# Sliding-window attention of a two-layer decoder: heads in pairs, one pair deeper, with the row maxima first

## The chip, the cores and the metric

The kernel is one program on one core of a Trainium2 chip. Its engines are TensorE (PE in the profile, with its weight loads as PEld), VectorE (DVE), ScalarE (ACT), GpSimd (POOL) and SyncE (SP), which issues DMAs. Each engine runs its own instructions in the order in which they are written; between engines they are ordered by semaphores. The metric is the time of one execution on the device in microseconds, of which the median over the runs is given; lower is better.

## The reference

Two layers run over a prompt of 128 tokens and a sample of 512 tokens, 1024 wide. The even layer mixes two branches: attention over 8 query heads of 64 with 2 key heads, and a gated delta rule in 4 heads of 128. The change is in the attention branch and in the norm of the delta branch that is computed beside it:

```python
def softmax_sink(s, sink, groups, rep):
    ...
    m = jnp.maximum(jnp.max(s, axis=-1, keepdims=True), sk)
    e = jnp.exp(s - m)
    return e / (jnp.sum(e, axis=-1, keepdims=True) + jnp.exp(sk - m))
```

A sample token sees the 128 context keys and the sample keys at most one block of 128 away, so a tile of 128 query tokens has 3 or 4 key tiles; the prompt tile (dense_attention) has one, its own. The product with the values goes, beside `rmsnorm(ob, out_norm) * silu(gate_b)` of the delta branch, into the output projection `w_out`. The odd layer and both feed-forward parts are not touched.

## The kernel before

All matrices stand with channels on the partitions and the 644 token columns (both sequences with gaps) along the free axis. Dense projections are split in a high and a low part and take three matmuls each. The order of each engine's work is written out by hand.

Even attention is one stage, which PE enters when the delta rule has ended and leaves for the output projection (`out_halves(0)`). It goes over 5 token tiles (`ATT`: four of the sample, then the prompt), 8 heads each, 40 units `u` in all (`ALLU`). A unit has these steps:

- `att_scores` (PE, L2555): scores of two heads at once, the two halves of the rows, into PSUM banks 0 and 1. It waits until the row maximum of the last unit has been taken (`a_rowmax`).
- L1801 (DVE): adds the mask, writes `scores` and takes the row maximum with the sink in one pass; L1805 makes the negative scaled maximum (`a_max`).
- L1110 (ACT): the exponential into `probs`, with the row sum; L1112 (ACT): the exponential of the sink of this one head.
- `att_turn` (PE, L2201 through the helper `turn`): 128x128 transposes into bank 2 or 3; `att_copy_a` (ACT, L493): copies them to `probs_t`.
- `att_values` (PE, L2578): product with the values, into bank 4 or 5 by the unit's parity.
- `att_scale` (DVE, L1780, L1781, L1786): denominator, reciprocal, and scaling of 64 columns into `o_attn`, for each unit.
- After 8 units `att_out` turns `o_attn` (PE), ACT writes `h_hi` (L1101), DVE `h_lo` (L1792).

`scores`, `probs` and `probs_t` have two buffers each, by the unit's parity. Beside this run the delta branch's norms, placed by `on_head(u, step)` from `ON_AT`: a square (ACT L1078), two statistics of ones times squares (PE L2544), two logarithms and exponentials (ACT L1086, L1091), two gated products (DVE L1753, L1758), `h_hi` (ACT L1095) and `h_lo` (DVE L1764) for each of 4 heads. At the entry two weight blocks of the output projection are split (ACT L782, DVE L1366), and the last rows of the modulation are turned. `keep_busy(b, n)` (L2203) issues n matmuls of 256 columns on constants whose result nobody reads.

In PE's loop before, step u issues the scores (even u, for u and u+1), then the transposes of u-1, then the values of u-2, then any norm statistic.

Of the kernel before, what the change touches and what calls it, by code (L numbers as in the profile page):

```python
# [26 lines left out]
P = 128  # L27
# [81 lines left out]
def build(nc, a, outs):  # L109
# [344 lines left out]
    ON_AT = [4 + 8 * h for h in range(B_HEADS)]  # L454
# [101 lines left out]
    with stack:  # L556
# [217 lines left out]
        def _(act):  # L774
# [328 lines left out]
            for u, (t, h) in enumerate(ALLU):  # L1103
                s = u % 2
                c0, c1 = att_local(t)
                act.wait_ge(S("a_max"), u + 1)
                if u >= 2:
# [13 lines left out]
                if u % 8 == 3 and t != ATT[0]:  # L1121
                    att_out(ATT.index(t) - 1, "oa_hi")
            att_copy_a(act, len(ALLU) - 1)
# [228 lines left out]
        def _(dve):  # L1352
# [395 lines left out]
            def on_step(u):  # L1748

                h = on_head(u, 6)  # L1750
# [4 lines left out]
                h = on_head(u, 7)  # L1755
# [3 lines left out]
                h = on_head(u, 9)  # L1759
# [15 lines left out]
            def att_scale(u):  # L1775

                t, h = ALLU[u]
                i = ATT.index(t)
                dve.wait_ge(S("a_sink"), u + 1)
                step(dve.tensor_tensor(ASM[:, u:u + 1], ASM[:, 128 + u:129 + u], ASM[:, 192 + u:193 + u], ALU.add))  # L1780
                step(dve.reciprocal(ASM[:, u:u + 1], ASM[:, u:u + 1]))  # L1781
                dve.wait_ge(S("a_pv"), u + 1)
                if u % 8 == 0 and i >= 2:
                    dve.wait_ge(S("oa_turned"), i - 1)
                q0 = (4 + u % 2) * 512 + 64 * h
                dve.tensor_scalar(OA[i % 2][:, 64 * h:64 * h + 64], PS[:, q0:q0 + 64], ASM[:, u:u + 1], None, ALU.mult  # L1786
# [8 lines left out]
            for u, (t, h) in enumerate(ALLU):  # L1795
                s = u % 2
# [13 lines left out]
                if u == 0:  # L1810
# [3 lines left out]
                if u in (3, 4):  # L1814
                    w_rest(N0_EVEN_OUT + u - 3)
                if 5 <= u < 12:
                    i = u - 4
                    gains(i // 4, i // 2 % 2, 1 + i % 2)
                on_step(u)
            att_scale(len(ALLU) - 2)  # L1820
            att_scale(len(ALLU) - 1)
# [178 lines left out]
        def _(pe):  # L2000
# [526 lines left out]

            for c in range(2):
# [5 lines left out]
            def on_stat(u):  # L2534

                for hf in range(2):
                    h = on_head(u, 1 + 2 * hf)
# [30 lines left out]
            def att_values(u):  # L2568
# [3 lines left out]
                if u >= 2:  # L2572

                    pe.wait_ge(S("oa_scaled"), u - 1)
                out = PS[:, (4 + u % 2) * 512 + 64 * h:(4 + u % 2) * 512 + 64 * h + 64]
# [6 lines left out]
            def att_out(i):  # L2582
                pe.wait_ge(S("oa_scaled"), 8 * (i + 1))
# [6 lines left out]
            for u in range(len(ALLU) + 2):  # L2590
                if u < len(ALLU) and u % 2 == 0:
                    att_scores(u)
                if 1 <= u <= len(ALLU):
                    att_turn(u - 1)
                if u >= 2:
                    att_values(u - 2)
                if u == 1:
                    mod_turn(MROUNDS + 1, MROW, 7)
                on_stat(u)
                if u == len(ALLU) - 7:  # L2600
                    pe.wait_ge(*of("ln", "on", 8))
                if u >= len(ALLU) - 7:
                    keep_busy(7, 1)
                if u % 8 == 3 and u > 8:
                    att_out(u // 8 - 1)
# [206 lines left out]
```

## Time and profile before

| | us |
|---|---|
| median of 3 runs | 1928.52 |
| lowest, highest run | 1926.64, 1929.06 |
| the profiled execution: its time | 1928.23 |
| its span | 1926.4 |
| PE busy, of the span | 1841.1 (96%) |
| DVE busy | 963.8 (50%) |
| ACT busy | 827.9 (43%) |
| chain that ended last, by engine | PE 85%, DVE 6%, ACT 4%, issue 3%, DMA 1% |
| mean granted clock of TensorE | 0.993 |

Busy shares are averages over stages with different limits; the stage of the change is 98 us of the span, from 438.2 to 536.2 us. A granted clock of 1.00 is 2.4 GHz, 0.50 is 1.2 GHz. In the chain of waits each piece is what the next one waited for; "issue" is time in which an engine waited for nothing that the profile shows.

### The profile page before, as it was taken

The numbers are of one execution on the slowest core, as the hardware profiler recorded it, in microseconds if no ns is written. First come the engines' busy times: TensorE is split into PE (matmuls) and PEld (weight loads), VectorE is DVE, ScalarE is ACT, GpSimd is POOL, SyncE is SP. The second block draws the span as 40 slices with busy tenths as digits, with TensorE's granted clock in tenths as the row PEclk, the third lists the DMA queues.
The fourth block names the chain that finished last, engine by engine and source line by source line (L and its number), as shares of the span: only waits on it lengthen the run. The fifth ranks groups of instructions, "written<-read, shape, count | busy, mean of one in ns | idle before, by whom it ended". The sixth has DMA issues, their size and how long they took to land.

```text
span 1926.4 us, 36263 instructions
## 1 busy us (share of the span) xinstructions
PE 1841.1 (96%) x14824; PEld 1698.8 (88%) x14824; DVE 963.8 (50%) x1613; ACT 827.9 (43%) x1420; POOL 55.0 (3%) x76
## 2 busy tenths in 40 slices
PE   6999998888899999999999999999999999999998
PEld 3999966667799999999999887776899999999997
DVE  4433355556746655235555743344375553255555
ACT  4545422225745544124445653343464441244453
POOL 0000122220000000000000000000000000000000
PEclk9999999998999999999999999999999999999999
DMA  7222366531021223222234311110211232122243
GB/s 284 65 58 66 128 252 221 199 141 51 1 71 44 77 71 87 71 66 68 73 94 140 95 44 32 27 35 28 67 44 55 76 87 78 55 76 76 78 136 115
DMA packets 238723, 170.23 MB, mean 88 GB/s; under 512 B 20139, under 2 KB 230285, under 8 KB 232333
## 3 DMA queue, kind: packets, MB, share of 16 engines
q1 hardware_dynamic: 238604, 168.54, 28.2%
q8 instruction: 88, 1.44, 0.3%
q14 instruction: 31, 0.25, 0.0%
HBM read 165.08 MB, written 3.44 MB: 87 GB/s over the span
## 4 chain that ended last, share of the span: by engine, by line
PE 85%; DVE 6%; ACT 4%; issue 3%; DMA 1%; SPq 0%; ACTq 0%; DVEq 0%
PE ps L2007 46%; PE ps L2083 15%; PE ps L2040 4%; PE ps L2201 3%; PE ps L2708 2%; PE ps L2745 2%; PE ps L2704 2%; PE ps L2398 1%; PE ps L2220 1%; PE ps L2578 1%; PE ps L2451 1%; PE ps L2555 1%; PE ps L2211 1%; PE ps L2028 1%; ACT w_hi L782 1%
## 5 line engine op out<-in xcount | busy, mean ns | idle before, releaser
L782 ACT ACTIVATE w_hi<-w_raw 128x1024 fp32r<-128x1024 f32 (+4 forms) x187 | 198.6, 1062 | 559.6 <-PE ps L2007 436.0
L1366 DVE TENSOR_TENSOR w_lo<-w_raw,w_hi 128x1024 fp32r<-128x1024 f32 (+4 forms) x191 | 234.2, 1227 | 377.2 <-ACT w_hi L782 376.8
L2007 PE MATMUL ps<-h_hi,w_hi 128*128 128x322 f32 x1648 | 381.5, 313 | 3.2 <-ACT conv L972 1.7
L2007 PE MATMUL ps<-h_lo,w_hi 128*128 128x322 f32 x1648 | 380.2, 312 | 0.0
L2007 PE MATMUL ps<-h_hi,w_lo 128*128 128x322 f32 x1648 | 378.1, 310 | 0.0
L2007 PEld LDWEIGHTS ps<-h_hi,w_hi 128*128 128x128 f32 x1648 | 278.1, 189 | 4.8 <-ACT conv L1192 2.0
L2007 PEld LDWEIGHTS ps<-h_hi,w_lo 128*128 128x128 f32 x1648 | 279.1, 189 | 0.0
L2007 PEld LDWEIGHTS ps<-h_lo,w_hi 128*128 128x128 f32 x1648 | 279.1, 189 | 0.0
L2083 PE MATMUL ps<-g_hi,w_hi 128*128 128x322 f32 x352 | 110.7, 314 | 2.7 <-DVE g_lo L1850 1.6
L2083 PE MATMUL ps<-g_lo,w_hi 128*128 128x322 f32 x352 | 109.6, 311 | 0.0
L2083 PE MATMUL ps<-g_hi,w_lo 128*128 128x322 f32 x352 | 109.1, 310 | 0.0
L2083 PE MATMUL ps<-h_hi,w_out_hi 128*128 128x322 f32 x288 | 90.8, 315 | 0.0
L2083 PE MATMUL ps<-h_lo,w_out_hi 128*128 128x322 f32 x288 | 89.8, 312 | 0.0
L2083 PE MATMUL ps<-h_hi,w_out_lo 128*128 128x322 f32 x288 | 89.5, 311 | 0.0
L1837 DVE SCALAR_TENSOR_TENSOR conv<-u,vec_cols,conv 128x642 f32<-128x642 f32 x88 | 78.0, 886 | 12.5 <-ACT conv L1192 12.1
L1840 DVE SCALAR_TENSOR_TENSOR conv<-u,vec_cols,conv 128x642 f32<-128x642 f32 x88 | 78.1, 887 | 10.6 <-DVE conv L1837 0.6
L1197 ACT ACTIVATE g_hi<-gated 128x642 f32 (+1 forms) x44 | 32.6, 741 | 104.0 <-DVE gated L1848 104.0
L2083 PEld LDWEIGHTS ps<-g_hi,w_hi 128*128 128x128 f32 x352 | 66.3, 188 | 4.0 <-DVE g_lo L1850 2.2
L1192 ACT ACTIVATE conv<-ps,vec_cols 128x644 f32<-128x644 f32 x88 | 69.7, 792 | 0.0
L2083 PEld LDWEIGHTS ps<-g_lo,w_hi 128*128 128x128 f32 x352 | 66.4, 189 | 0.2
L2083 PEld LDWEIGHTS ps<-g_hi,w_lo 128*128 128x128 f32 x352 | 66.5, 189 | 0.0
L1868 DVE COPY f_t<-ps 128x644 f32 (+1 forms) x16 | 13.3, 829 | 100.9 <-PE ps L2007 82.3
(376 smaller groups left out, 3337.5 us busy)
## 6 DMA issues: line engine op xcount, KB each, us to landing
w_raw<-in_ffn_w_up SPq DMA_DIRECT2D x88, 512.0 KB, 3.7
w_mod_raw<-in_w_mod SPq DMA_DIRECT2D x40, 1024.0 KB, 6.9
w_raw<-in_ffn_w_down SPq DMA_DIRECT2D x48, 704.0 KB, 4.5
w_raw<-in_ev_w_in SPq DMA_DIRECT2D x18, 512.0 KB, 3.6
w_mod_first<-in_w_mod SPq DMA_DIRECT2D x8, 1024.0 KB, 15.6
w_raw<-in_ev_w_out SPq DMA_DIRECT2D x8, 512.0 KB, 4.3
w_raw<-in_od_w_out SPq DMA_DIRECT2D x8, 512.0 KB, 4.0
w_raw<-in_od_w_kv_up SPq DMA_DIRECT2D x24, 128.0 KB, 2.3
```

The lines of the kernel that those rows point to most:

```text
L782: act.activation(WH[slot][:, 0:k, :], RAW[slot][:, 0:k, :], ACT.Copy).then_inc(w_hi, 1)
L1192: act.activation(halves(Y[b][:, :]), pair(b0 + 2 * slot), ACT.Copy, scale=vcol(v0 + b * FCH, j)).then_inc(evac_a, 1)
L1366: dve.tensor_tensor(WL[slot][:, 0:k, :], RAW[slot][:, 0:k, :], WH[slot][:, 0:k, :].bitcast(F32), ALU.subtract).then_inc(w_lo, 1)
L1837: dve.scalar_tensor_tensor(y[:, 1:643], u[:, 0:642], vcol(v0 + b * FCH, j), y[:, 1:643], ALU.mult, ALU.add).then_inc(S(f"f_conv{b}"), 1)
L1840: last = dve.scalar_tensor_tensor(y[:, 1:643], u[:, 2:644], vcol(v0 + b * FCH + 4 * FCH, j), y[:, 1:643], ALU.mult, ALU.add)
L2007: last = pe.matmul(out, w_of(k, wi), x_of(k, xi, i), start=(k == 0 and p == 0), stop=(k == ks - 1 and p == 2))
L2040: last = pe.matmul(bank(2 * slot + hf, HW), (WH, WL)[wi][slot][:, k, :], x[xi][:, k, hf * HW:(hf + 1) * HW], start=(k == 0 and p == 0), st ...
L2083: last = pe.matmul(out, w[wi][:, k, :], x[xi][:, k, tk(g)], start=(k == 0 and p == 0), stop=(k == ks - 1 and p == 2))
L2201: return pe.transpose(out, src, IDENT[0:rows, 0:rows])
L2704: return pe.matmul(area(s, k0, w), QPE[i % 2][half(s), tile], KPT[half(s), k0:k0 + w], start=True, stop=False)
L2708: return pe.matmul(area(s, k0, w), QN[h][:, tile], KN[h][:, k0:k0 + w], start=False, stop=True)
L2745: last = pe.matmul(COUT[:, P * s:P * s + P], VO[i % 2][:, s, kt_tile, :], pt, start=(x == 0), stop=(x == len(tiles) - 1))
```

## The change

1. PE goes over pairs of units. Iteration i issues the scores of pair i, the values of pair i-2, and the transposes of pair i-1, so the values lie one pair later than the transposes.
2. DVE takes both row maxima of a pair first, and does what else it has afterwards.
3. Denominators, reciprocals and scaling are done once for a tile of 8 heads: one subtraction (sink minus maximum) on DVE, one exponential of 8 columns on ACT (L1124 of the changed kernel), one addition, one reciprocal and one product of 512 columns on DVE. The values of a tile go all to one bank, 4 or 5 by the tile's parity.
4. ACT copies the transposes of unit u-2 after the exponential of unit u (before: of u-1).
5. The norm steps of the delta branch are placed anew (`ON_AT` from 2, steps further apart).
6. `keep_busy(7, 4)` is issued before PE's wait for the delta rule's last output, behind a new wait on `a_rotated`, and again behind the first scores. At the last four iterations 2 unread matmuls stand for each pair, as before 1 for each unit.

The diff, cut to its core:

```diff
-    ON_AT = [4 + 8 * h for h in range(B_HEADS)]
+    ON_AT = [2 + 8 * h for h in range(B_HEADS)]
+    NPAIR = len(ALLU) // 2
+    def a_max_at(u):
+        return S("a_max"), u + 1 + u // 8
...
-                    h = on_head(u, 2 + 2 * hf)
+                    h = on_head(u, 4 + 4 * hf)
...
-                    h = on_head(u, 3 + 2 * hf)
+                    h = on_head(u, 5 + 4 * hf)
...
-                h = on_head(u, 8)
+                h = on_head(u, 12)
...
                 act.activation(PR[s][:, c0:c1], SM[s][:, c0:c1], ACT.Exp, bias=ASM[:, 64 + u:65 + u],
                                scale=A_HD ** -0.5, accum_out=ASM[:, 128 + u:129 + u]).then_inc(S("a_exp"), 1)
-                act.activation(ASM[:, 192 + u:193 + u], SNK[:, h:h + 1], ACT.Exp, bias=ASM[:, 64 + u:65 + u]
-                               ).then_inc(S("a_sink"), 1)
-                if u >= 1:
-                    att_copy_a(act, u - 1)
+                if u % 8 == 7:
+                    i = u // 8
+                    act.wait_ge(S("a_max"), 9 * (i + 1))
+                    act.activation(ASM[:, 192 + 8 * i:200 + 8 * i], ASM[:, 192 + 8 * i:200 + 8 * i], ACT.Exp, scale=A_HD ** -0.5
+                                   ).then_inc(S("a_sink"), 1)
+                if u >= 2:
+                    att_copy_a(act, u - 2)
...
-                if u % 8 == 3 and t != ATT[0]:
-                    att_out(ATT.index(t) - 1, "oa_hi")
+                if u % 8 == 6 and u > 8:
+                    att_out(u // 8 - 1, "oa_hi")
...
-            def att_scale(u):
+            def att_scale(i):
...
+                dve.wait_ge(S("a_pv"), 8 * (i + 1))
...
+                dve.tensor_tensor(OA[i % 2][:, :].rearrange("p (g c d) -> p g c d", g=2, c=4),
+                                  bank(4 + i % 2).rearrange("p (g c d) -> p g c d", g=2, c=4),
+                                  den.rearrange("p (c g) -> p g c", g=2).unsqueeze(3).broadcast_to([P, 2, 4, 64]), ALU.mult
...
-                if u >= 2:
-                    att_scale(u - 2)
-                if u % 8 == 4 and t != ATT[0]:
-                    att_lo(ATT.index(t) - 1)
+                if u % 2 == 0:
+                    continue
+                if u % 8 == 7:
+                    dve.tensor_tensor(by_unit(ASM, i, 192), ...
+                if u % 8 == 3 and u > 8:
+                    att_scale(i - 1)
+                if u % 8 == 7 and u > 8:
+                    att_lo(i - 1)
...
+            pe.wait_ge(S("a_rotated"), NT)
+            keep_busy(7, 4)
             for c in range(2):
                 pe.wait_ge(*both("o_done", c, NT))
...
-            for u in range(len(ALLU) + 2):
-                if u < len(ALLU) and u % 2 == 0:
+            for i in range(NPAIR + 2):
+                u = 2 * i
+                if i < NPAIR:
                     att_scores(u)
-                if 1 <= u <= len(ALLU):
+                if i == 0:
+                    keep_busy(7, 4)
+                if i >= 2:
+                    att_values(u - 4)
+                    att_values(u - 3)
+                if 1 <= i <= NPAIR:
+                    att_turn(u - 2)
                     att_turn(u - 1)
...
+                if i >= 18:
+                    keep_busy(7, 2)
+                if i % 4 == 2 and i > 4:
+                    att_out(i // 4 - 1)
```

Where the instructions now stand, at three places. First PE at the stage's entry, in the kernel before. L2525 is the delta rule's last product, L2555 the first scores, L2201 the transposes of `probs` and of the modulation's rows:

```order
L2525 MATMUL ps<-v_beta_165,k_state_183 128x128 x4
L2555 MATMUL ps<-qa_ka_va 128x128 [waits k_out_rows,k_attn,a_roped,o_done]
L2555 MATMUL ps<-qa_ka_va 128x128
L2555 MATMUL ps<-k_ctx_cols,qa_ka_va 128x128 x2
L2555 MATMUL ps<-qa_ka_va 128x128 x2
L2201 MATMUL ps<-consts,probs_194 128x128 [waits a_exp]
L2201 MATMUL ps<-consts,probs_194 128x128 x2
L2201 MATMUL ps<-consts,mod_rows 128x128 [waits mod_rows]
L2201 MATMUL ps<-consts,mod_rows 128x128 x3
L2555 MATMUL ps<-qa_ka_va 128x128 [waits a_rowmax]
```

And in the changed kernel, where L2543, L2575 and L2219 are the same three and L2224 the unread matmuls:

```order
L2543 MATMUL ps<-v_beta_165,k_state_183 128x128 x4
L2224 MATMUL ps<-consts 128x256 [waits a_rotated]
L2224 MATMUL ps<-consts 128x256 x3
L2575 MATMUL ps<-qa_ka_va 128x128 [waits k_out_rows,k_attn,a_roped,o_done]
L2575 MATMUL ps<-qa_ka_va 128x128
L2575 MATMUL ps<-k_ctx_cols,qa_ka_va 128x128 x2
L2575 MATMUL ps<-qa_ka_va 128x128 x2
L2224 MATMUL ps<-consts 128x256 x4
L2575 MATMUL ps<-qa_ka_va 128x128 [waits a_rowmax]
L2575 MATMUL ps<-qa_ka_va 128x128
L2575 MATMUL ps<-k_ctx_cols,qa_ka_va 128x128 x2
L2575 MATMUL ps<-qa_ka_va 128x128 x2
L2219 MATMUL ps<-consts,probs_194 128x128 [waits a_exp]
```

Four unread matmuls stand ahead of the first scores and four behind them; the second pair's scores have moved ahead of the first transposes.

Then PE over one pair in the middle of the stage, for a tile with 4 key tiles, before (L2578 are the values):

```order
L2555 MATMUL ps<-qa_ka_va 128x128 [waits a_rowmax]
L2555 MATMUL ps<-qa_ka_va 128x128 x3
L2555 MATMUL ps<-k_ctx_cols,qa_ka_va 128x128 x2
L2555 MATMUL ps<-qa_ka_va 128x128 x2
L2201 MATMUL ps<-consts,probs_195 128x128 [waits a_pt,a_exp]
L2201 MATMUL ps<-consts,probs_195 128x128 x3
L2578 MATMUL ps<-v_attn_tok,probs_t_196 128x64 [waits oa_scaled,a_pt]
L2578 MATMUL ps<-v_attn_tok,probs_t_196 128x64 x3
L2201 MATMUL ps<-consts,probs_194 128x128 [waits a_pt,a_exp]
L2201 MATMUL ps<-consts,probs_194 128x128 x3
L2578 MATMUL ps<-v_attn_tok,probs_t_197 128x64 [waits oa_scaled,a_pt]
L2578 MATMUL ps<-v_attn_tok,probs_t_197 128x64 x3
```

And in the changed kernel, where L2597 are the values:

```order
L2575 MATMUL ps<-qa_ka_va 128x128 [waits a_rowmax]
L2575 MATMUL ps<-qa_ka_va 128x128 x3
L2575 MATMUL ps<-k_ctx_cols,qa_ka_va 128x128 x2
L2575 MATMUL ps<-qa_ka_va 128x128 x2
L2597 MATMUL ps<-v_attn_tok,probs_t_196 128x64 [waits a_pt]
L2597 MATMUL ps<-v_attn_tok,probs_t_196 128x64 x3
L2597 MATMUL ps<-v_attn_tok,probs_t_197 128x64 [waits a_pt]
L2597 MATMUL ps<-v_attn_tok,probs_t_197 128x64 x3
L2219 MATMUL ps<-consts,probs_194 128x128 [waits a_pt,a_exp]
L2219 MATMUL ps<-consts,probs_194 128x128 x3
L2219 MATMUL ps<-consts,probs_195 128x128 [waits a_pt,a_exp]
L2219 MATMUL ps<-consts,probs_195 128x128 x3
```

Before, the second transpose of the row lies behind scores that were issued a few instructions earlier; now the transposes are of the pair before, behind the values of the pair before that.

Last ACT over one pair, before (L1110 exponential, L1112 the sink's, L493 copy, L1101 the tile's `h_hi`), in the second token tile:

```order
L1110 ACTIVATE probs_194,attn_small<-scores_192,attn_small 128x512 [waits a_turned,a_max]
L1112 ACTIVATE attn_small<-sink_b,attn_small 128x1
L493 ACTIVATE probs_t_197<-ps 128x512 [waits a_pv,a_turned]
L1110 ACTIVATE probs_195,attn_small<-scores_193,attn_small 128x512 [waits a_turned,a_max]
L1112 ACTIVATE attn_small<-sink_b,attn_small 128x1
L493 ACTIVATE probs_t_196<-ps 128x512 [waits a_pv,a_turned]
L1101 ACTIVATE h_hi<-ps 128x4x128 [waits oa_turned]
L1110 ACTIVATE probs_194,attn_small<-scores_192,attn_small 128x512 [waits a_turned,a_max]
L1112 ACTIVATE attn_small<-sink_b,attn_small 128x1
```

And in the changed kernel (L1119 exponential, L502 copy, L1095 logarithm, L1104 and L1110 the two writes of `h_hi`, L1124 the sinks of 8 heads, L1100 the norm's exponential), at the last pair of the second tile:

```order
L1119 ACTIVATE probs_194,attn_small<-scores_192,attn_small 128x512 [waits a_turned,a_max]
L502 ACTIVATE probs_t_196<-ps 128x512 [waits a_pv,a_turned]
L1095 ACTIVATE on_rstd_211<-ps,eps 128x322 [waits norm_stat]
L1104 ACTIVATE h_hi<-o_delta 128x644 [waits on_gated]
L1110 ACTIVATE h_hi<-ps 128x4x128 [waits oa_turned]
L1119 ACTIVATE probs_195,attn_small<-scores_193,attn_small 128x512 [waits a_turned,a_max]
L1124 ACTIVATE attn_small<-attn_small 128x8 [waits a_max]
L502 ACTIVATE probs_t_197<-ps 128x512 [waits a_pv,a_turned]
L1100 ACTIVATE on_rstd_211<-on_rstd_211 128x322 [waits norm_ln]
```

What belongs to the norms and to `h_hi` stands now between the first copy and the second exponential of a pair, three instructions of it in this one.

## Rows read from the trace of the kernel before

In the views by stretch the columns are the stretch and its length, then for PE, PEld, DVE, ACT and POOL the busy us with the count of instructions in brackets, then the granted clock of TensorE, the share of DMA and GB/s. In the groups by line they are line, engine, operation, shapes and count, then busy us and mean ns of one, then the idle us before them and what ended it.

**Rows 1.** Busy time by stretch, one row for each token tile

```profile
438.20:460.05 21.85, 20.13 (x115) 17.16 (x117) 12.25 (x49) 12.26 (x35) 0.28 (x6) 0.61 0.21 61
460.05:480.47 20.42, 17.98 (x165) 14.97 (x164) 14.52 (x56) 15.12 (x42) 0.00 (x0) 1.00 0.01 2
480.47:501.14 20.67, 18.75 (x171) 15.65 (x170) 13.92 (x52) 14.81 (x41) 0.00 (x0) 1.00 0.01 2
501.14:518.98 17.84, 15.76 (x136) 12.66 (x135) 12.94 (x52) 13.22 (x41) 0.00 (x0) 1.00 0.00 1
518.98:536.19 17.21, 14.94 (x86) 10.01 (x86) 12.26 (x59) 10.81 (x41) 0.00 (x0) 1.00 0.01 1
```

**Rows 2.** Busy time by stretch, at the stage's entry and around 1081 us

```profile
436.80:438.20 1.40, 0.01 (x1) 0.00 (x0) 1.29 (x2) 0.00 (x0) 0.00 (x0) 1.00 0.64 193
438.20:439.20 1.00, 0.94 (x12) 0.78 (x12) 0.00 (x0) 0.00 (x0) 0.28 (x6) 1.00 0.77 236
439.20:440.80 1.60, 0.00 (x0) 0.00 (x0) 1.56 (x5) 0.74 (x3) 0.00 (x0) 0.86 0.07 19
440.80:457.40 16.60, 16.58 (x88) 14.59 (x88) 8.96 (x36) 9.27 (x25) 0.00 (x0) 0.50 0.22 64
1081.00:1084.00 3.00, 0.78 (x4) 0.49 (x3) 1.73 (x3) 2.94 (x6) 0.00 (x0) 1.00 0.17 50
```

**Rows 3.** Chain of waits over one pair of heads (start, length, what)

```profile
475.12 1.12 PE ps L2555 x16
...
476.26 0.75 DVE scores L1801
...
478.11 0.66 PE ps L2201 x4
...
478.77 1.10 PE ps L2578 x8
479.88 0.60 PE ps L2544 x2
480.47 0.53 PE ps L2555 x5
```

**Rows 4.** Timeline of ACT, one head (start, length, engine, line, operation)

```profile
479.03 0.71 ACT L1110 ACTIVATE probs<-scores,attn_small 128x512 f32<-128x512 f32 x1
479.64 0.19 ACT L1110 ACTIVATION_READ_ACCUMULATOR probs<-scores,attn_small 128x1 f32 x1
...
479.74 0.29 ACT L1112 ACTIVATE attn_small<-sink_b,attn_small 128x1 f32<-128x1 f32 x1
479.92 0.58 ACT L493 ACTIVATE probs_t<-ps 128x512 f32<-128x512 f32 x1
...
480.40 0.47 ACT L1091 ACTIVATE on_rstd<-on_rstd 128x322 f32<-128x322 f32 x1
```

**Rows 5.** Groups by line and form on ACT, 438.2 to 536.2 us

```profile
L1110 ACT ACTIVATE probs<-scores,attn_small 128x384 f32<-128x384 f32 x16 | 9.8, 613 | 16.7 <-DVE attn_small L1805 16.7
...
L493 ACT ACTIVATE probs_t<-ps 128x384 f32<-128x384 f32 x16 | 7.5, 469 | 0.0
...
L1086 ACT ACTIVATE on_rstd<-ps,eps 128x322 f32<-128x322 f32 x8 | 4.1, 516 | 0.0
...
L1101 ACT ACTIVATE h_hi<-ps 128x512 fp32r<-128x512 f32 x5 | 2.9, 589 | 1.9 <-PE ps L2201 1.9
L1078 ACT ACTIVATE on_sq<-o_delta 128x644 f32<-128x644 f32 x4 | 2.9, 727 | 0.0
...
L782 ACT ACTIVATE w_hi<-w_raw 128x1024 fp32r<-128x1024 f32 x2 | 2.1, 1042 | 0.0
```

**Rows 6.** Groups by line and form on DVE, same stretch (busy, mean ns, idle)

```profile
L1786 DVE TENSOR_SCALAR o_attn<-ps,attn_small 128x64 f32<-128x64 f32 x40 | 11.3, 284 | 12.7 <-PE ps L2578 11.9
...
L1792 DVE TENSOR_TENSOR h_lo<-ps,h_hi 128x512 fp32r<-128x512 f32 x5 | 3.4, 683 | 1.4 <-ACT h_hi L1101 1.4
```

**Rows 7.** Chain of waits, the kernel's two unread matmuls at the stage's end

```profile
534.72 0.86 PE ps L2206 x4
```

More of the change, by code:

```diff
@@ L453, in build, with by_unit @@
     A_ROPE = (4, 0, 1, 2, 3)
-    ON_AT = [4 + 8 * h for h in range(B_HEADS)]
+    ON_AT = [2 + 8 * h for h in range(B_HEADS)]
+    NPAIR = len(ALLU) // 2
+    def a_max_at(u):
+        return S("a_max"), u + 1 + u // 8
+    def by_unit(m, i, first=0):
+        return m[:, first + 8 * i:first + 8 * i + 8].rearrange("p (c g) -> p c g", g=2)
     def on_head(u, step):
@@ L1120, in _ @@
                 on_step(u)
-                if u % 8 == 3 and t != ATT[0]:
-                    att_out(ATT.index(t) - 1, "oa_hi")
-            att_copy_a(act, len(ALLU) - 1)
+                if u % 8 == 6 and u > 8:
+                    att_out(u // 8 - 1, "oa_hi")
+            for u in (len(ALLU) - 2, len(ALLU) - 1):
+                att_copy_a(act, u)
             att_out(NT - 1, "oa_hi")
@@ L1748, in on_step @@
             def on_step(u):
-                h = on_head(u, 6)
+                h = on_head(u, 10)
                 if h is not None:
@@ L1773, in rope @@
                 return dve.tensor_tensor(dst, dst, ROT[:, :], ALU.add)
-            def att_scale(u):
[L1777 to L1783, printed above, removed]
+            def att_scale(i):
+                dve.wait_ge(S("a_sink"), i + 1)
+                den = ASM[:, 8 * i:8 * i + 8]
+                step(dve.tensor_tensor(den, ASM[:, 128 + 8 * i:136 + 8 * i], ASM[:, 192 + 8 * i:200 + 8 * i], ALU.add))
+                step(dve.reciprocal(den, den))
+                dve.wait_ge(S("a_pv"), 8 * (i + 1))
+                if i >= 2:
                     dve.wait_ge(S("oa_turned"), i - 1)
-                q0 = (4 + u % 2) * 512 + 64 * h
-                dve.tensor_scalar(OA[i % 2][:, 64 * h:64 * h + 64], PS[:, q0:q0 + 64], ASM[:, u:u + 1], None, ALU.mult
+                dve.tensor_tensor(OA[i % 2][:, :].rearrange("p (g c d) -> p g c d", g=2, c=4),
+                                  bank(4 + i % 2).rearrange("p (g c d) -> p g c d", g=2, c=4),
+                                  den.rearrange("p (c g) -> p g c", g=2).unsqueeze(3).broadcast_to([P, 2, 4, 64]), ALU.mult
                                   ).then_inc(S("oa_scaled"), 1)
@@ L1813, in _ @@
                     mod_out(MROUNDS - 1)
[L1814 to L1821, printed above, removed]
+                if u in (3, 5):
+                    w_rest(N0_EVEN_OUT + u // 2 - 1)
+                for x in (u - 1, u):
+                    if 5 <= x < 12:
+                        j = x - 4
+                        gains(j // 4, j // 2 % 2, 1 + j % 2)
+                    on_step(x)
+            att_scale(NT - 1)
             att_lo(NT - 1)
@@ L2571, in att_values @@
                 pe.wait_ge(S("a_pt"), u + 1)
-                if u >= 2:
-                    pe.wait_ge(S("oa_scaled"), u - 1)
-                out = PS[:, (4 + u % 2) * 512 + 64 * h:(4 + u % 2) * 512 + 64 * h + 64]
+                if i >= 2:
+                    pe.wait_ge(S("oa_scaled"), i - 1)
+                out = PS[:, (4 + i % 2) * 512 + 64 * h:(4 + i % 2) * 512 + 64 * h + 64]
                 tiles = att_tiles(t)
@@ L2582, in att_out @@
             def att_out(i):
-                pe.wait_ge(S("oa_scaled"), 8 * (i + 1))
+                pe.wait_ge(S("oa_scaled"), i + 1)
                 if i:
@@ L2588, in att_out @@
                 last.then_inc(S("oa_turned"), 1)
-            for u in range(len(ALLU) + 2):
-                if u < len(ALLU) and u % 2 == 0:
+            for i in range(NPAIR + 2):
+                u = 2 * i
+                if i < NPAIR:
                     att_scores(u)
-                if 1 <= u <= len(ALLU):
+                if i == 0:
+                    keep_busy(7, 4)
+                if i >= 2:
+                    att_values(u - 4)
+                    att_values(u - 3)
+                if 1 <= i <= NPAIR:
+                    att_turn(u - 2)
                     att_turn(u - 1)
-                if u >= 2:
-                    att_values(u - 2)
-                if u == 1:
+                if i == 1:
                     mod_turn(MROUNDS + 1, MROW, 7)
                 on_stat(u)
-                if u == len(ALLU) - 7:
+                on_stat(u + 1)
+                if i == 18:
                     pe.wait_ge(*of("ln", "on", 8))
[L2602 to L2605, printed above, removed]
+                if i >= 18:
+                    keep_busy(7, 2)
+                if i % 4 == 2 and i > 4:
+                    att_out(i // 4 - 1)
             att_out(NT - 1)
```

14 lines of the change are left out of this document (8 added, 6 removed).

## The prediction, made before the changed kernel ran

> **What bounds the kernel now.** I read the busy time by stretch first, one stretch for each token tile, cut where PE begins a tile's first scores [rows 1]. The stage takes 21.85 + 20.42 + 20.67 + 17.84 + 17.21 = 98.0 us of the 1926.4. PE is busy for 88 to 92% of each stretch, DVE and ACT for 56 to 75%: no engine is full, so the limit is a round of waits. The first stretch is the odd one: three key tiles for each query tile, as in the fourth, yet 4 us longer, at a mean granted clock of 0.61.
>
> The same view cut finer at the entry [rows 2] shows why. PE idles 1.40 us, works 0.94, idles 1.60, and then the clock is at 0.50 (1.2 GHz) for 16.60 us, in which PE is busy without a pause. So in the entry PE bounds, at half speed.
>
> Next the chain of waits over a pair of heads at full clock [rows 3]. It goes scores 1.12, DVE's pass 0.75 and its small steps, ACT's exponential, transposes 0.66, values 1.10, a norm statistic 0.60, and the next scores begin at 480.47, 5.35 us after the last. Ahead of the transposes at 478.11 PE waits for ACT: the scores are issued only just ahead of what needs them. That round trip is what the deeper order takes away.
>
> Behind the stage PE works without a gap into the output projection, and all that follows starts from the end of this stage. So I carry the stage's gain one to one to the end.
>
> **The change part by part.** One round per pair is left: a pair's first transposes on PE release ACT's exponential, then come ACT's copy, the second exponential, the second copy, then PE's values of the second head, and behind these, in PE's order, the next pair's first transposes. Scores and row maxima lie beside it. ACT's timeline [rows 4] gives its parts by starts: exponential 479.03 to 479.74 = 0.71 (the sink's exponential then took 0.18 more, and goes), copy 479.92 to 480.40 = 0.48, its whole length 0.58. Round: 0.66 + 0.71 + 0.48 + 0.71 + 0.58 + 1.10 = 4.24; transposes behind other matmuls are a little shorter, so 4.2 with the handovers. Before, a pair took 5.35 with a statistic.
>
> But ACT's other work lies inside this round when it stands between the first copy and the second exponential, where the order of the changed kernel has it. Its lengths [rows 5] less the 0.10 that successive ones overlap by [rows 4]: square 0.63, logarithm 0.42, `h_hi` of the norm 0.63 (as wide as the square), `h_hi` of the tile 0.49, the sinks' one exponential 0.20. One pair in a tile has square and logarithm, 1.05; another has logarithm, both writes and the sinks, 1.74. The norm's exponential (0.46) stands behind the second copy, where PE's values cover it.
>
> Third tile (four key tiles): 4 x 4.2 + 1.05 + 1.74 = 19.6, and 0.5 more where a statistic (0.60) and the tile's transposes meet in a pair in which PE, not ACT, ends last: 20.1, for 20.67 now. Second tile: the round that opens it still has the small values and transposes (0.22 less for each of three or four groups, together 1.0) and no `h_hi` writes (1.12): 18.0, for 20.42. Fourth: it opens with a full round, 4.2 + 1.74; then three of 3.45 (exponential 0.61 and copy 0.37 by [rows 5], a quarter off PE's parts), one with 1.05 more, and 0.5: 17.8, for 17.84. So the middle of the stage gains 3.0 in all: the order removes 1.1 us of waiting per pair and ACT's row of small jobs gives most of it back.
>
> Entry. Four unread matmuls cost 2 x 0.86 = 1.72 [rows 7] against 1.40 of idle time [rows 2]: the scores begin 0.3 later. If the clock stays: scores 0.94, four unread 1.72 (beside DVE's two maxima), scores 0.95. Then ACT's list sets the pace, from 0.9 later (one maximum): exponential 0.61, copy 0.37, a weight split 0.94, square 0.63, exponential 0.61, copy 0.37 = 3.5; then values, two groups of transposes and the statistic, 2.0; then one round on PE, 2.9. Sum 0.3 + 3.6 + 6.4 + 2.9 = 13.2, for 21.85. I take the clock as held: all but 0.1 of the idle stretches that the fall followed is filled. The bound on the other side is a fall all the same, 19 to 22 us (below).
>
> End. PE enters it with one more pair of values owing: 17.2 + 1.65 (two values of three key tiles, 0.75 x 1.10 each) + 0.86 (two unread matmuls of one more iteration) + 0.40 (DVE's product of 512 columns instead of 64) = 20.1. The trace has no product with a broadcast operand of this shape; it lies between the 64-column one (0.28) and twice the 0.68 of the subtraction, 1.4; I take 0.68, as the subtraction of 512 columns from PSUM [rows 6]. Only the last tile's is uncovered. The other four lie on DVE between maxima: two passes of 0.75 with their small steps fill about half of a round of 4.2, and scaling adds its 0.68 and two small ones. Forty additions, reciprocals and small products go from DVE; it was not the bound, so they are worth nothing by themselves.
>
> Added waits: `oa_scaled` ahead of a tile's first values is set two tiles earlier; DVE's wait for a tile's last values comes behind both maxima of a pair, and the maxima behind it have a round's time. DVE's wait for the tile's `h_hi` at a tile's last pair holds back the next maxima by up to 3 us, within ACT's 5.9 us round. PE's `a_rotated` is met before the idle time starts. SP's and POOL's work is as before.
>
> Sum: 13.2 + 18.0 + 20.1 + 17.8 + 20.1 = 89.2, against 98.0: 8.8 less. The profiled execution took 1928.23 (span 1926.4, 1.8 around it), 0.3 under the median 1928.52. So 1919.4 for it, and **1919.7** for the median.
>
> One row of this sum has a page beside it. The sink's exponential for one head took 0.29 [rows 4], and I keep that for the one of 8 columns. The Trainium skill, "ScalarE: Activation LUTs", section "What ACT_TABLE_LOAD costs", has a bias read from memory cost some 93 ns, and an ACTIVATE with immediate operands 186 ns plus 0.83 ns a column; the new one has no such bias. By the page it is an estimate of 0.19, and the sum 0.5 lower at most.
>
> **The rivals.** First, PE bounds and ACT's jobs are covered. For it: PE is busy 18.75 of 20.67 us in the third tile and 15.76 of 17.84 in the fourth [rows 1], and these are the times that a filled PE would need at most. 12.5 + 17 + 18.75 + 15.8 + 16.5 = 80.6: 1911. Against it: values, then transposes, stand in PE's order behind the copy, and only a round with no ACT jobs in it is under PE's own length. The Trainium skill, "TensorE: Matmul & The Clock Gate", section "Architectural detail: the array is 16× 32×32, not 1× 128×128", says that PE may pull weight loads ahead but not matmuls, and that ACT and DVE are strictly first in, first out; by that rule nothing shortens the round, so it speaks for the forecast. No row here tests it.
>
> Second, the clock falls once, at the entry in spite of the filling, or in one of four later rounds in which PE waits some 2 us for ACT (5.9 less about 3.9 of work). At the entry: the first idle time is gone and the second pair's scores come early, 19.5 instead of 21.85, 6.3 above my term: 1926.0. For it: the fall came after gaps of 1.40 and 1.60 us with 0.94 of work between [rows 2]. Against: with 0.78 us of work in 3 us around 1081 the clock stayed at 1.00 [rows 2].
>
> Third, slower: it falls twice. A fall costs up to half of the 16.6 us at 0.50 [rows 2]; I take 7. 1919.7 + 14 = 1933.7. It decides from the second fall on: one alone leaves the kernel at 1926 to 1927.
>
> Fourth, the deeper order takes no wait away, because DVE, held by its wait for `h_hi`, delivers the maxima late in every tile: another 1 us or so for each tile and a longer end, 1926.
>
> **How the numbers follow.** Forecast 0.55; PE bound 0.10; one fall 0.20; two falls 0.10; maxima late 0.05. The range 1911 to 1928 leaves out the two falls and the far end of the first rival; the forecast's own is 1916 to 1923. 0.2% of the time is 3.9 us, about what a measurement of this kernel can tell from no change: faster means under 1924.7. Forecast, PE bound and a third of the one-fall case (a late or short one) are faster, 0.72; the rest of that case and the fourth are the same, 0.18; two falls are slower, 0.10.
>
> **What would show it.** Right: a granted clock of 1.00 from 434 to 536 us; the second tile's scores near 451; rounds of about 4.2 us, and near 5.9 where ACT has both `h_hi` writes, with PE released there by `probs_t` before the second head's values; an output projection starting near 527.5. Wrong: 0.50 anywhere in the stage; PE released by `attn_small` or `a_rowmax` in most pairs; rounds as long without ACT's jobs as with them; or an end stretch well off 20 us.

## The result: 0.26% slower, where 0.5% faster was predicted

The changed kernel takes **1934.91 us**, the median of 12 runs (1929.24 to 1940.93). The kernel before took 1928.13 beside it (12 runs, 1925.50 to 1932.28); the ratio on record is 1.0026, 95% interval [1.0014, 1.0038] (the two medians alone give 1.0035). The prediction was 1919.7, its range 1911 to 1928: wrong in sign and outside the range. What happened is what the third rival named, with a chance of 0.10 and 1933.7 us: the clock falls more than once.

The profiled execution took 1940.93, the longest of the twelve (span 1938.9, mean clock 0.987; before 1926.4 and 0.993). So it shows where time was lost, and more of it than the median execution lost. The stretches of the changed kernel's stage, one for each token tile, with the columns of [rows 1]:

```profile
441.55:459.30 17.75, 16.16 (x105) 13.51 (x104) 9.42 (x32) 8.51 (x20) 0.07 (x3) 0.73 0.26 75
459.30:480.07 20.77, 19.65 (x159) 17.41 (x158) 10.39 (x34) 11.31 (x31) 0.00 (x0) 0.82 0.00 1
480.07:505.27 25.20, 22.39 (x170) 19.61 (x168) 11.21 (x32) 13.37 (x33) 0.00 (x0) 0.80 0.01 2
505.27:523.55 18.28, 15.25 (x139) 13.19 (x138) 10.14 (x32) 12.16 (x33) 0.00 (x0) 1.00 0.00 1
523.55:547.51 23.96, 19.62 (x101) 15.34 (x101) 11.11 (x38) 13.01 (x44) 0.00 (x0) 0.79 0.00 1
sum 105.96, PE 93.07 PEld 79.05 DVE 52.27 ACT 58.35 POOL 0.07; mean PE 18.61 PEld 15.81 DVE 10.45 ACT 11.67 POOL 0.01
```

The stage takes 106.0 us instead of 98.0. The column to read is the granted clock, third from the end: before, only the first tile was under 1.00 (0.61); now four of five are. The one that is not, the fourth, takes 18.28, for a forecast of 17.8. The same view cut at the falls:

```profile
449.00:466.00 17.00, 16.14 (x80) 14.03 (x80) 7.10 (x26) 7.87 (x23) 0.00 (x0) 0.52 0.21 62
466.00:483.00 17.00, 15.21 (x147) 13.33 (x146) 8.61 (x27) 10.64 (x26) 0.00 (x0) 0.98 0.01 2
483.00:490.00 7.00, 5.97 (x30) 5.10 (x32) 2.86 (x8) 3.82 (x11) 0.00 (x0) 0.56 0.00 1
...
497.00:500.00 3.00, 3.00 (x17) 3.00 (x18) 1.98 (x5) 0.96 (x4) 0.00 (x0) 0.58 0.00 0
...
528.00:538.00 10.00, 9.79 (x41) 7.66 (x40) 5.04 (x20) 4.81 (x20) 0.00 (x0) 0.51 0.00 0
```

Four falls to 0.50 (1.2 GHz) where there was one. Three more lie outside the stage, which the kernel before's profile did not have:

```profile
289.00:296.00 7.00, 6.24 (x62) 3.19 (x61) 1.42 (x5) 0.00 (x0) 0.00 (x0) 0.52 0.66 243
333.00:337.00 4.00, 4.00 (x59) 1.65 (x54) 0.95 (x4) 0.00 (x0) 0.00 (x0) 0.58 0.79 270
1094.00:1098.00 4.00, 3.25 (x8) 2.48 (x9) 2.32 (x3) 3.94 (x9) 0.00 (x0) 0.60 0.26 67
```

The kernel before's profile has one outside too, at 30 to 37 us, which the changed kernel's has not. Between them the first scores start at 441.55 instead of 438.23; the entry's unread matmuls account for 0.2 us of that. The change touches nothing there; a second profile of the kernel before shows that such falls come and go (experiment 11).

What PE was doing when the clock fell, just before 484, is in the timeline of the third tile's opening pair (start, length, engine, operation; in brackets the idle time before it and what ended it). It answers to [rows 3, 4]:

```profile
481.06 0.52 ACT L1095 ACTIVATE on_rstd<-ps,eps 128x322 f32<-128x322 f32 x1
481.22 1.10 PE L2597 MATMUL ps<-v_attn_tok,probs_t 128*128 128x64 f32 x8
481.47 0.73 ACT L1104 ACTIVATE h_hi<-o_delta 128x644 fp32r<-128x644 f32 x1
482.10 0.59 ACT L1110 ACTIVATE h_hi<-ps 128x512 fp32r<-128x512 f32 x1
482.58 0.72 ACT L1119 ACTIVATE probs<-scores,attn_small 128x512 f32<-128x512 f32 x1
482.73 0.69 DVE L1805 TENSOR_TENSOR h_lo<-ps,h_hi 128x512 fp32r<-128x512 f32 x1 [3.35 <-ACT h_hi L1110]
...
483.28 0.21 ACT L1124 ACTIVATE attn_small<-attn_small 128x8 f32<-128x8 f32 x1
...
483.38 0.59 ACT L502 ACTIVATE probs_t<-ps 128x512 f32<-128x512 f32 x1
...
484.03 1.76 PE L2597 MATMUL ps<-v_attn_tok,probs_t 128*128 128x64 f32 x7 [1.70 <-ACT probs_t L502]
484.07 0.74 DVE L1814 CUSTOM_DVE_ANT_0 scores<-ps,consts,sink_scaled 128x512 f32<-128x512 f32 x1
```

PE ends the first head's values at 482.32 and idles 1.70 us. ACT meanwhile runs logarithm, both `h_hi` writes, exponential, the sinks and the second copy, in the order of the forecast. The second head's values then take 1.76 us for seven recorded matmuls, where the first head's eight took 1.10 just before: the clock has halved. The same lines show DVE idle for 3.35 us, waiting for `h_hi`, with the next pair's first maximum (L1814) behind it.

The other three falls also came at or soon after a wait of PE for that copy. In the list of PE's matmuls the number in brackets is the wait; the clock fell at 449.7, 497.5 and 528.2:

```profile
449.86 0.90 PE L2597 MATMUL ps<-v_attn_tok,probs_t 128*128 128x64 f32 x3 [1.32 <-ACT probs_t L502]
...
496.84 1.40 PE L2597 MATMUL ps<-v_attn_tok,probs_t 128*128 128x64 f32 x8 [1.11 <-ACT probs_t L502]
...
527.14 0.88 PE L2597 MATMUL ps<-v_attn_tok,probs_t 128*128 128x64 f32 x6 [1.72 <-ACT probs_t L502]
```

Summed over the stage by who waits for whom, first the changed kernel, then the kernel before (us, times, longest):

```profile
DVE h_lo L1805 <- ACT h_hi L1110: 12.4, 5, 3.3
PE ps L2597 <- ACT probs_t L502: 11.8, 10, 1.7
...
PE ps L2575 <- DVE attn_small L1814: 0.3, 1, 0.3
```

```profile
PE ps L2201 <- ACT probs L1110: 7.9, 13, 1.6
```

PE's old wait, its transposes for ACT's exponential (7.9 us in 13 waits), is gone as planned. In its place stands a wait for ACT's second copy, 11.8 us in 10, nearly 1.2 us each.

### The profile page after: what moved, and what is told of

It is laid out like the page before. It is cut to its first block, busy times and chain, and to the rows that moved or that the text cites. A ratio compares the mean times of both kernels' runs of the same rounds, so it can differ in the third digit from the quotient of the medians.

```text
span 1938.9 us, 36105 instructions
## 1 busy us (share of the span) xinstructions
PE 1850.8 (95%) x14838; PEld 1710.4 (88%) x14838; DVE 950.4 (49%) x1513; ACT 819.8 (42%) x1385; POOL 54.9 (3%) x76
## 4 chain that ended last, share of the span: by engine, by line
PE 86%; DVE 5%; ACT 5%; issue 2%; DMA 1%; SPq 0%; ACTq 0%; DVEq 0%
PE ps L2025 45%; PE ps L2101 15%; PE ps L2058 4%; PE ps L2219 3%; PE ps L2733 2%; PE ps L2770 2%; PE ps L2729 2%; PE ps L2597 2%; PE ps L2416 1%; PE ps L2238 1%; PE ps L2469 1%; ACT w_hi L791 1%; PE ps L2229 1%; PE ps L2575 1%; PE ps L2046 1%
```

## Experiments

Each was timed beside the kernel before, whose median there was 1929.4 (experiments 1 to 4), 1929.6 (5 to 8) or 1932.7 (9, 10, 12), so the ratios are the safer comparison. "Unread matmuls" compute what nobody reads. The medians are of 12 runs, or of 6 where it says so. Comments in the diffs of 1, 6, 7 and 8 are added here.

**1. Fill PE's waits for ACT.**

```diff
+                    keep_busy(2, {2: 5, 4: 1, 6: 2, 8: 5, 10: 2, 12: 5, 14: 2, 16: 5}.get(i, 0))   # between the two heads' values
```

> The changed kernel with 27 more unread matmuls of 256 columns (5, 1, 2, 5, 2, 5, 2, 5 of them in iterations 2, 4, 6 and so on to 16), put between the values of a pair's first and second head, where PE waits for ACT's second copy. Theory A (the order of the change takes about the time that was forecast for it, and what turned it round is TensorE's clock, which falls where PE waits 1.0 to 2.5 us for ACT in these rounds): the granted clock stays at 1.00 from the delta rule to the output projection, the stage takes 89 to 92 us, and the median is 1920 to 1923. Theory B (the clock is not the cause, the rounds themselves are too long): the unread matmuls add some of their 27 x 0.43 = 11.6 us, and the median is 1935 to 1945. In between, 1924 to 1934, the clock still falls at the entry only.

1927.94 us, ratio 0.9991 [0.9978, 1.0003]. Its stage, by tile:

```profile
443.90:457.90 14.00, 13.73 (x117) 11.66 (x116) 9.42 (x32) 8.24 (x20) 0.06 (x2) 1.00 0.31 94
457.90:475.90 18.00, 17.80 (x165) 15.31 (x164) 10.38 (x34) 11.64 (x31) 0.00 (x0) 1.00 0.01 3
475.90:496.50 20.60, 20.40 (x183) 18.07 (x182) 11.21 (x32) 13.32 (x33) 0.00 (x0) 1.00 0.01 2
496.50:515.00 18.50, 18.10 (x153) 15.62 (x152) 10.14 (x32) 12.15 (x33) 0.00 (x0) 1.00 0.00 1
515.00:535.26 20.26, 17.05 (x111) 13.73 (x111) 11.11 (x38) 13.02 (x44) 0.00 (x0) 1.00 0.00 1
sum 91.36, PE 87.09 PEld 74.38 DVE 52.25 ACT 58.36 POOL 0.06; mean PE 17.42 PEld 14.88 DVE 10.45 ACT 11.67 POOL 0.01
```

Adding 27 matmuls of no use takes 7.0 us off the median, and in the profile the clock holds through the stage. At full clock the tiles take 14.0, 18.0, 20.6, 18.5 and 20.3; the forecast had 13.2, 18.0, 20.1, 17.8 and 20.1. So the durations were nearly right, and the clock was the cost. The stage is where theory A put it (89 to 92 us), the median is above its 1920 to 1923: this execution, at 1930.20, still has some 20 us at half clock, all of them outside the stage.

**2. Without the unread matmuls at the entry.**

```diff
-            pe.wait_ge(S("a_rotated"), NT)
-            keep_busy(7, 4)
-                if i == 0:
-                    keep_busy(7, 4)
```

> The changed kernel without its two groups of four unread matmuls at the entry. Theory A: the clock falls at the entry with or without them, since the wait for ACT in the second round brings it down; the fall comes some 5 us earlier, the four matmuls behind the first scores (1.7 us) are saved: 1931 to 1937, no measurable difference from the changed kernel. Theory C (the unread matmuls do keep the clock up in most executions, and the profile showed a bad one): 3 to 8 us slower than the changed kernel, 1938 to 1943.

1933.51 us, 1.0018 [1.0002, 1.0034]: no slower than with them, as theory A has it.

**3. ACT's small jobs behind the second copy.** Only the place in ACT's order changes: the norm's steps, the two weight splits of the entry and the `h_hi` writes follow the copy of the second head instead of preceding its exponential.

```diff
-                if u in (2, 3):
...
-                    hi(N0_EVEN_OUT + u - 2)
+                if u % 2 == 0:
+                    continue
+                if u == 3:
...
+                on_step(u - 1)
                 on_step(u)
-                if u % 8 == 6 and u > 8:
+                if u % 8 == 7 and u > 8:
```

> The changed kernel with ACT's norm steps, weight splits and h_hi writes of each pair moved behind the pair's second copy, instead of between the first copy and the second exponential. Theory A: the second copy comes 1.0 to 1.7 us earlier in half of the rounds, PE's waits ahead of the second head's values shrink to under 0.5 us in them, the jobs are covered in part by PE's values; the clock stays up in most of the stage: 1916 to 1924. Theory B (other waits take their place, DVE's wait for h_hi above all, or the clock falls at the entry anyway): 1928 to 1936.

1934.75 us, 1.0019 [1.0000, 1.0039]: nothing gained, which was theory B. The waits of PE and DVE in its stage tell why:

```profile
PE ps L2580 <- DVE attn_small L1819: 9.0, 5, 2.4
PE ps L2602 <- ACT probs_t L502: 1.2, 5, 0.5
...
DVE h_lo L1810 <- ACT h_hi L1110: 17.8, 5, 5.0
```

The wait for `probs_t` is all but gone (11.8 to 1.2), and a new one of 9.0 us in 5 stands in its place: scores wait for DVE's maxima. `h_hi` is now written later, DVE waits for it longer (17.8 us in 5 waits, up to 5.0, for 12.4 and 3.3), and the maxima are queued behind. Four of the five waits last 2.05 to 2.41 us, and each was followed within 2 us by a fall of the clock (453, 484, 508, 528), 34 us at half clock in all.

**4. The kernel before with the entry's unread matmuls.** The two `keep_busy(7, 4)` of experiment 2 are added to the kernel before, the second after its first scores.

> The kernel before with only the unread matmuls of the entry (four ahead of the first scores, four behind them). Theory A: the old order keeps PE's waits under about 1 us in the first rounds, so filling the entry holds the clock there, where it now falls in the profile: the first tile takes 14 to 16 us instead of 21.85, and the median is 1921 to 1924. Rival D (the clock falls in the first tile anyway, a little later, as in the changed kernel): 1928 to 1930, with the 1.7 us of the second group added.

1928.12 us, 0.9996 [0.9980, 1.0011]: the same, where theory A had 1921 to 1924; rival D's time came. In its profile the entry has a fall of 3.4 us at 452 instead of 17 from 440, yet the median does not move.

**5. Both waits out of the way.** Experiment 3, and DVE writes a tile's `h_lo` one pair later (the norms' `h_lo` two units, its two weight splits one pair), so that its wait for `h_hi` is met before it gets there:

```diff
-                h = on_head(u, 13)
+                h = on_head(u, 15) if u < 39 else B_HEADS - 1
...
-                if u % 8 == 7 and u > 8:
-                    att_lo(i - 1)
+                if u % 8 == 1 and u > 16:
+                    att_lo(i - 2)
...
-                if u in (3, 5):
-                    w_rest(N0_EVEN_OUT + u // 2 - 1)
+                if u in (5, 7):
+                    w_rest(N0_EVEN_OUT + u // 2 - 2)
...
+            att_lo(NT - 2)
```

> The changed kernel with ACT's norm steps, weight splits and h_hi writes behind each pair's second copy, and besides DVE's h_lo of a tile one pair later, its h_lo of the norms two units later and its two weight splits one pair later, so that DVE's row maxima no longer stand behind its wait for ACT. Theory A (time = work at full clock plus what the clock's falls cost; PE's waits of over 2 us bring it down): the waits of 2.1 to 2.4 us that PE had for a row maximum in the kernel without the later h_lo are gone, the mean granted clock is back near 0.995, the stage takes 88 to 92 us where the clock stays up, median 1918 to 1925. Theory B (the deeper order loses the clock whatever the waits): clock 0.990, median 1931 or more.

**1917.35 us** (6 runs), 0.9928 [0.9909, 0.9947]: a little better than theory A. Its stage takes 82.0 us in the profile, under the 88 to 92 expected.

**6 and 7. Which fills matter.** Experiment 1 with the fills at the entry alone (pairs 2 and 4), and with the later ones alone (pairs 6 to 16).

```diff
+                    keep_busy(2, {2: 5, 4: 1}.get(i, 0))                                  # experiment 6
+                    keep_busy(2, {6: 2, 8: 5, 10: 2, 12: 5, 14: 2, 16: 5}.get(i, 0))      # experiment 7
```

> The changed kernel with unread matmuls in PE's wait for ACT in the entry's third and fifth rounds alone (5 and 1). Theory A: the falls in the entry go, those in the later tiles stay; half or more of what the 27 unread matmuls regained (6.9 us): 1929 to 1932, mean clock 0.992 to 0.994. Rival E (one fall draws the next, so that keeping the clock at the entry keeps it in the stage): 1926 to 1928.

> The changed kernel with unread matmuls in the waits of the later tiles alone (21 in rounds 6 to 16). Theory A: the entry falls as in the changed kernel, the later tiles keep the clock: 1929 to 1932. Rival E: as the changed kernel, 1933 to 1936, since the clock is already down when the later rounds come.

Entry alone 1935.46, 1.0023 [1.0008, 1.0039]; later ones alone 1927.75, 0.9988 [0.9973, 1.0003]. Filling the entry gains nothing, filling the later tiles gains the whole 7 us. Neither expectation named this: theory A had about half for each, rival E the reverse. In the profiles experiment 6 has five falls in the stage, all from the second tile on (469, 500, 514, 524, 531), experiment 7 one, at the entry (446). The waits in the later tiles are what costs.

**8. Filling the kernel before.** The kernel of experiment 4 with one more unread matmul in each of pairs 1 to 15.

```diff
+                    keep_busy(2, 1)   # ahead of the transposes of units 2, 4, ..., 30
```

> The kernel before with the unread matmuls of the entry, and one more ahead of the transposes of each pair's first head (15 of them), where PE waits for ACT. Theory A: the clock stays at 1.00 through the stage in nearly every execution; the stage takes 93 to 96 us, and the median is 1925 to 1928, one to three us under the kernel before. Rival F (its clock was lost outside the stage anyway, the filling only adds time): 1929 to 1932.

1927.87 us, 0.9988 [0.9973, 1.0003]: within theory A's 1925 to 1928, but no difference that can be told from none. The kernel before has little clock to win in its stage, 2 to 3 us by the table below.

**9. Experiment 5 without the entry's unread matmuls** (the edit of experiment 2).

> The kernel with ACT's small jobs behind the second copy and DVE's waits for h_hi one pair later (1917.35, stage 82.0 us), without the unread matmuls at the entry. Theory (the small jobs on the ring were the cost, the unread matmuls at the entry were worth nothing): 1915 to 1920, ratio 0.991 to 0.996 to the kernel before. Rival (the entry's unread matmuls keep the clock up through the first tile): a stretch at 0.50 at 440 to 460, 6 us more, about 1923, ratio near 0.997.

**1913.35 us** (6 runs, 1912.27 to 1918.95), 0.9897 [0.9881, 0.9914]: the lowest median, though its interval overlaps that of the same kernel with the entry's matmuls (experiment 12). The profiled execution is the slowest of the six; in it the first tile is at clock 0.75, the fall that the rival named, while the other five runs are all under 1914.6.

**10. DVE's part of experiment 5 alone**, with ACT's jobs left where the change has them.

> The changed kernel with DVE's waits for h_hi one pair later, but ACT's small jobs left between the first copy and the second exponential. Theory (both parts count; ACT's jobs on the ring hold PE and bring the clock down, whatever DVE does): PE still waits for probs_t 1 to 2 us in rounds with jobs, stage 96 to 106 us, time 1930 to 1936, ratio 1.000 to 1.003. Rival (DVE's late maxima were the true cost, ACT's place is nothing): stage near 84 us, time near 1918, ratio 0.993 to 0.995.

1935.86 us, 1.0028 [1.0012, 1.0045], as the theory has it. Its PE waits, and below them the longest of PE's with both parts (profile of experiment 12):

```profile
PE ps L2598 <- ACT probs_t L502: 12.9, 12, 1.7
PE ps L2576 <- DVE attn_small L1814: 0.3, 1, 0.3
```

```profile
PE ps L2603 <- ACT probs_t L502: 2.0, 7, 0.5
```

The same wait as in the changed kernel, and next to none for DVE. So neither part gains anything by itself (experiments 3 and 10), and the two together gain 17 to 20 us by the medians (experiments 5 and 12). DVE's wait for `h_hi` was hidden behind ACT's jobs; moving the jobs alone lengthened it and laid it bare.

**11. The kernel before, profiled once more** (a single execution, 1931.26 us).

> The kernel before, profiled once more. Theory (its fall of the clock at the entry of the stage in the first profile is one of several places where it can fall, and not in every execution there): another set of stretches at 0.50; if none lies at 440 to 457, the stage takes about 92 us instead of 98. Rival (the fall at the entry belongs to the kernel before in every execution): again some 17 us at 0.50 from 440, stage near 98.

Falls lie at 29 to 36, 381 to 387, 442 to 449, 1084 and 1166. Its stage:

```profile
441.04:460.20 19.16, 15.60 (x115) 12.79 (x115) 12.25 (x49) 12.52 (x36) 0.28 (x6) 0.82 0.24 70
460.20:480.70 20.50, 18.06 (x164) 15.06 (x163) 14.52 (x56) 14.68 (x40) 0.00 (x0) 1.00 0.01 2
480.70:501.40 20.70, 18.79 (x171) 15.68 (x170) 13.91 (x52) 14.85 (x41) 0.00 (x0) 1.00 0.00 1
501.40:519.20 17.80, 15.73 (x134) 12.63 (x133) 12.93 (x52) 13.18 (x40) 0.00 (x0) 1.00 0.01 1
519.20:536.48 17.28, 15.01 (x87) 10.08 (x86) 12.25 (x59) 10.89 (x41) 0.00 (x0) 1.00 0.01 1
```

Tiles 2 to 5 repeat [rows 1] to 0.2 us. The first takes 19.16, not 21.85, since its fall lasts 7 us, not 17. The stage's 95.4 us lie between the theory's 92 and the rival's 98: the entry's fall came again, much shorter. The 17 us in [rows 2] were one execution's, not the kernel's. Two profiles are too few for a mean.

**12. Experiment 5 once more.**

> The kernel with ACT's small jobs behind the second copy and DVE's waits one pair later, once more, since it had only six runs. Theory: 1915 to 1920, ratio 0.991 to 0.996. Rival (the six runs happened to have few falls of the clock): median 1922 to 1927, ratio 0.997 to 0.999, at a lower mean clock than 0.9955.

**1914.77 us** (6 runs), 0.9902 [0.9881, 0.9924], at the theory's lower end. Its stage, all at full clock:

```profile
440.87:453.50 12.63, 11.78 (x105) 9.79 (x104) 8.97 (x30) 8.05 (x20) 0.07 (x2) 1.00 0.21 62
453.50:470.10 16.60, 16.46 (x160) 14.53 (x158) 11.01 (x37) 11.92 (x31) 0.00 (x0) 1.00 0.12 35
470.10:487.90 17.80, 17.56 (x169) 15.64 (x168) 11.35 (x32) 13.34 (x33) 0.00 (x0) 1.00 0.01 3
487.90:503.60 15.70, 15.25 (x139) 13.20 (x138) 10.32 (x32) 12.05 (x33) 0.00 (x0) 1.00 0.00 1
503.60:521.27 17.67, 15.39 (x101) 11.93 (x101) 11.01 (x38) 12.79 (x44) 0.00 (x0) 1.00 0.01 1
sum 80.40, PE 76.44 PEld 65.08 DVE 52.65 ACT 58.16 POOL 0.07; mean PE 15.29 PEld 13.02 DVE 10.53 ACT 11.63 POOL 0.01
```

PE is busy 16.46 of 16.60 and 17.56 of 17.80 us in tiles 2 and 3: PE bounds there. It is the first rival's stage, for which the prediction had 80.6; it takes ACT's jobs off the round and DVE's wait out of the way to get there.

**The clock's price over all runs.** Each run lists its time and mean granted clock. A fit through the 207 timed runs, with one slope and an offset for each kernel, gives 1.48 us for each 0.001 of mean clock, and what a kernel would take at a clock of 1.00 throughout. That last is an extrapolation, not a run; the runs scatter by 1.4 us around the fit:

| kernel | mean time | mean clock | at 1.00 |
|---|---|---|---|
| before (81 runs) | 1930.6 | 0.9943 | 1922.1 |
| changed | 1934.6 | 0.9900 | 1919.8 |
| changed, waits filled (1) | 1927.8 | 0.9951 | 1920.6 |
| changed, entry not filled (2) | 1933.5 | 0.9897 | 1918.3 |
| changed, entry's waits filled (6) | 1934.6 | 0.9909 | 1921.2 |
| changed, later waits filled (7) | 1927.7 | 0.9948 | 1919.9 |
| before, entry filled (4) | 1928.9 | 0.9954 | 1922.1 |
| before, entry and pairs filled (8) | 1928.0 | 0.9962 | 1922.3 |
| ACT's jobs moved alone (3) | 1933.6 | 0.9897 | 1918.4 |
| DVE's wait moved alone (10) | 1936.6 | 0.9895 | 1921.1 |
| both (5) | 1917.4 | 0.9955 | 1910.7 |
| both (12) | 1914.5 | 0.9963 | 1909.1 |
| both, entry not filled (9) | 1914.3 | 0.9957 | 1907.9 |

Of what experiments 5, 9 and 12 gain on the changed kernel, 9 to 12 us are there at full clock and 8 to 9 us are clock.

The profiles place the loss. Time at half clock within the stage is 38, 24, 34, 20 and 17 us where the later waits stand (changed, experiments 2, 3, 6, 10), and 0, 3, 3, 7 and 0 us where they are filled or gone (1, 5, 7, 9, 12). Outside the stage there is no such order: 10 to 14 us in the first five, 7 to 34 in the others.

## Why the prediction was wrong, step by step

**The failed step: "I take the clock as held."** It was argued for the entry alone. The forecast's own rounds of 5.9 us, of which PE works 3.9, leave about 2 us of waiting in each later tile; the prediction named them, in the second rival, and gave one fall 0.20 and two 0.10. In the profiled execution there were four in the stage. By the table the change gains 2.3 us at full clock (1922.1 to 1919.8) and loses 0.0043 of mean clock, 6.3 us at 1.48 for each 0.001: 4.0 slower, as the means of the table have it. (Beside the 12 runs of the kernel before that were timed with it, the mean is 6.2 slower; for those no clock is on record.) Experiments 1, 6 and 7 show the cause and not only the sum: filling the later waits gives 7 us back, filling the entry gives none.

The forecast's 1919.7 is also what the table has for the changed kernel at full clock, 1919.8. That is in part luck: the forecast keeps the fall at 30 to 37 us of the profile it started from, the table's figure has none.

**Second, what there was to gain.** Of the 8.8 us forecast, 8.7 were the first tile's (21.85 to 13.2), nearly all of it the fall of [rows 2]. That fall was taken as a property of the kernel, since the profiled execution lay on the median. It is not one: in the second profile of the kernel before it lasts 7 us instead of 17, and filling that kernel's entry leaves its median where it was (experiment 4). The execution of [rows 1] had few falls elsewhere and a long one there, so its total looked ordinary.

**The durations at full clock: right.** Second tile 18.0 for 18.0, third 20.1 for 20.6, fourth 17.8 for 18.5, end 20.1 for 20.3, entry 13.2 for 14.0 (forecast, then experiment 1). Sum 91.4 instead of 89.2; experiment 1's unread matmuls may have a part in these 2.2 us, which no run here separates. Two slips in the working change little: PE's busy share in the last stretch is 87%, not 88 to 92, and the fourth tile's parts add up to rounds of 3.38, not 3.45, 0.2 us over three of them.

**Small terms.** The product with the broadcast operand, taken as 0.68 between 0.28 and 1.4, takes 0.69; the sinks' one exponential, kept at 0.29, takes 0.21:

```profile
L1797 DVE TENSOR_TENSOR o_attn<-ps,attn_small x5: 691/692/692, 470.1 to 544.6; 128x512 f32<-128x512 f32 x5
L1124 ACT ACTIVATE attn_small<-attn_small x5: 197/208/208, 460.8 to 542.2; 128x8 f32<-128x8 f32 x5
```

The second one is near the estimate of 0.19 from the Trainium skill, "ScalarE: Activation LUTs", section "What ACT_TABLE_LOAD costs".

**First rival** (PE bounds, 1911): not in the changed kernel, but it is what experiments 5, 9 and 12 are. The argument against it, that ACT's jobs stand inside the round, was right, and moving them was what remained to be done.

**Third rival**: happened. Its 1933.7 lies near the median by luck as well as by mechanism. Its price was 7 us for each of two falls, added to a forecast that had the kernel before's fall taken out; in the profiled execution the four stretches of the stage are 17, 7, 3 and 10 us long, and together they make the stage 14.6 us longer than that of experiment 1 (106.0 against 91.4).

**Fourth rival**, DVE's wait for `h_hi` makes the maxima late: dismissed as "within ACT's 5.9 us round". That is right of the changed kernel, whose PE waits for DVE for 0.3 us. But the wait hid behind ACT's jobs, and experiment 3 brought it out at once.

**What stays open.** Why the clock falls outside the stage (near 30, 250, 290, 333, 381, 1084, 1166) in some executions and not in others of the same kernel. Also whether the deeper order or the batched denominators and scaling make the 2.3 us at full clock; they were not tried apart.

## What to carry to other kernels

Work that stands in an in-order engine's queue between two steps of a ring can cost nearly its full length in every round, even if that engine is idle for a third of the time: here the jobs add up to 10 or 11 us over four tiles by the prediction's lengths (1.05 and 1.74 a tile), and the stage without them on the ring is 11.0 us shorter at full clock (80.4 against experiment 1's 91.4, which has its unread matmuls too). Put such work behind the last step that the ring waits for, and then check each engine that waits for the moved work, since one wait can hide behind another and then neither edit gains anything alone. Count the clock as part of the price of a wait: ten gaps under 2 us on PE cost more here than the gain that brought them. And do not take a fall of the clock in one profile for the kernel's; look at several executions, or at the mean clock of all the runs, before forecasting what its removal is worth.

## What the runs showed of the hardware

- In the changed kernel's stage the four falls to 0.50 began in the last 0.2 us of an idle stretch of PE (1.32 us before 449.86, 1.70 before 484.03) or 0.7 and 1.1 us after one (1.11 before 496.84, 1.72 before 527.14). In the fourth tile a stretch of 1.71 us before 509.19 was followed by none: the clock stayed at 1.00 until 528.
- Being busy did not end a fall at once: from 449 to 466 PE worked for 16.14 of 17.00 us, in [rows 2] for 16.58 of 16.60, before full clock was granted again.
- A stretch at half clock lasted from about 3 to 17 us in these profiles. At 1.48 us for each 0.001 of mean clock, much of the kernel before's spread, 1923 to 1939 us, goes with the clock.
